# A hybrid decoder step: first block reordered, output projection's router and decode tile and the delta stage's decode products on column tiles

## The reference

```python
hn = rms_norm(x, norm1_g) * (1 + sc1) + sh1          # sh, sc, gt: silu(c) @ w_ada + b_ada
qkv, z, beta, alpha, u = split(hn @ w_in)
q, k, v = split(silu(causal_conv(qkv)))              # 4 heads of 128; q, k normalized
o, s_gdn = gdn_chunked(q, k, v, -exp(a_log) * softplus(alpha + dt_bias), sigmoid(beta), s0)
o_a = rms_norm(o) * silu(z)
y, x_s5 = s5_scan(u, x0, ...)                        # 32 groups of 64 complex states
y = gelu(y); o_b = rms_norm(y * sigmoid(y @ glu_w + glu_b))
x = x + gt1 * (concat(o_a, o_b) @ w_out)
hn = rms_norm(x, norm2_g) * (1 + sc2) + sh2
s = sigmoid(hn @ w_router)                           # 16 experts in 4 groups: best group, top 2 in it
x = x + gt2 * sum_e combine_e * (silu(hn @ w_gate_e) * (hn @ w_up_e)) @ w_down_e
y = rms_norm(x, final_g)
```

## Time and profile before

| | |
|---|---|
| time, median of 3 runs | 1298.97 us (1297.41 to 1302.08) |
| the profiled execution | 1299.72 us, its span 1298.0 us |
| granted PE clock, mean | 0.926 |
| busy: PE, PEld, DVE, ACT, POOL | 1121.2 (86%), 680.7 (52%), 552.8 (43%), 306.5 (24%), 230.6 (18%) us |

### The profile page before, as it was taken

One profiled execution on the slowest core, in us unless ns is written; L12 is line 12 of the kernel. 1 busy time (PEld: TensorE's weight loads), 2 busy tenths in 40 slices (PEclk: granted clock), 3 DMA queues, 4 the chain that ended last, 5 costly groups with the idle time before them and its releaser, 6 DMA issues. The chain is left out here.

```text
span 1298.0 us, 15179 instructions
## 1 busy us (share of the span) xinstructions
PE 1121.2 (86%) x5094; PEld 680.7 (52%) x5095; DVE 552.8 (43%) x1238; ACT 306.5 (24%) x684; POOL 230.6 (18%) x366
## 2 busy tenths in 40 slices
PE   4899997996996899688879799996499999889876
PEld 3466664444865677577764445543244444434332
DVE  3143357275365354697732432546411111111128
ACT  5121231051113333322214222232011111101123
POOL 0100000085403334211120000102311111101050
PEclk9899999997998996888889899997699999999988
DMA  9587061011015000375517100006377565797463
GB/s 349 167 245 259 1 258 65 1 66 65 14 26 132 2 1 1 126 282 172 171 33 284 66 17 32 33 33 156 101 259 259 166 216 172 243 319 262 146 258 149
DMA packets 127007, 181.95 MB, mean 140 GB/s; under 512 B 36685, under 2 KB 80450, under 8 KB 126942
## 3 DMA queue, kind: packets, MB, share of 16 engines
q1 hardware_dynamic: 115948, 146.96, 34.1%
q0 software_dynamic: 7376, 21.59, 5.0%
q10 hardware_dynamic: 3626, 12.64, 2.4%
HBM read 131.62 MB, written 48.47 MB: 139 GB/s over the span
## 5 line engine op out<-in xcount | busy, mean ns | idle before, releaser
L2128 PE MATMUL bank<-w_out,H 128*128 x384 | 173.4, 605 | 11.3 <-DMA w_out<-in_w_up 6.4
L368 PE MATMUL bank<-hT,w_ring 128*128 128x344 f32 x576 | 170.9, 459 | 3.8 <-ACT hT L552 3.8
L368 PEld LDWEIGHTS bank<-hT,w_ring 128*128 128x128 f32 x576 | 110.5, 193 | 62.6 <-issue 6.4
L2128 PEld LDWEIGHTS bank<-w_out,H 128*128 128x128 f32 x384 | 72.9, 193 | 109.2 <-issue 109.2
L2408 PE MATMUL bank<-w_out,hT 128*128 128x512 f32 (+1 forms) x288 | 127.5, 595 | 0.5 <-DVE hT L1920 0.5
L453 PE MATMUL bank<-w_ring,hT 128*128 128x512 f32 x256 | 115.1, 606 | 8.8 <-issue 8.8
L2192 DVE TENSOR_TENSOR H<-H,bank 128x256 f32<-128x256 f32 x24 | 10.1, 420 | 248.2 <-ACT H L2163 248.2
L2112 PE MATMUL bank<-y1T,H 128*128 x192 | 91.4, 620 | 10.6 <-DVE H L2201 7.9
L453 PEld LDWEIGHTS bank<-w_ring,hT 128*128 128x128 f32 x256 | 64.4, 256 | 55.1 <-issue 41.7
L2408 PEld LDWEIGHTS bank<-w_out,hT 128*128 128x128 f32 (+1 forms) x288 | 50.1, 179 | 64.5 <-issue 63.7
L2112 PEld LDWEIGHTS bank<-y1T,H 128*128 128x128 f32 x192 | 35.5, 195 | 52.3 <-issue 52.3
(11 more groups left out here) (523 smaller groups left out, 1797.3 us busy)
## 6 DMA issues: line engine op xcount, KB each, us to landing
ys_d<-ZO SPq DMA_DIRECT2D x18, 1024.0 KB, 13.1
y1T<-in_w_down SPq DMA_DIRECT2D x16, 1024.0 KB, 5.6
w_out<-in_w_gate SPq DMA_DIRECT2D x16, 1024.0 KB, 8.1
w_out<-in_w_up SPq DMA_DIRECT2D x16, 1024.0 KB, 11.5
ys_d<-H ACTq DMA_DIRECT2D x24, 512.0 KB, 5.4
w_ring<-in_w_in SPq DMA_DIRECT2D x4, 2048.0 KB, 8.2
y1T<-in_w_ada SPq DMA_DIRECT2D x4, 2048.0 KB, 8.1
hT<-in_w_ada SPq DMA_DIRECT2D x4, 2048.0 KB, 13.0
```

The source lines that it names most:

```text
L368: mm = t.matmul(ps[3 * (m % 2) + s][:, 0:SEG], w_ring[:, q % 2, k, (m % 4) * P:(m % 4 + 1) * P], hT[:, k, s * SEG:(s + 1) * SEG], start=(k ...
L2128: mm = t.matmul(ps[2 + p][:, :], xT[p][:, k, :], wgu[:, bass.ds(buf, 1), k, :].rearrange("p o n -> p (o n)"), start=(k == 0), stop=(k == K ...
```

## The change

*First block.* The second half of `powers` now follows the copies of the gate rows, and the first two phase tables are made ahead of the wait for the gates. *Delta stage.* `decode_product` takes all four heads at once; each head writes its own 32 partitions of bank 3 (a column tile of PE), and the loop runs over tokens outside, heads inside. Two calls take the place of four. ACT's `product_rows` first copies the four pieces to their places and then scales them. *Row products* become transposes. *Output projection.* The tiles go in the order 0, 1, 2, decode, 3 to 7. The router's eight products write four column tiles: the weights, loaded twice so that 32 columns are filled, are held and the tokens streamed; ACT copies the partial sums out (`lg_part`), and one product with `pick16` adds them and turns them back (`logits`), in the middle of the next half tile. The decode tile is made the same way, from the last 32 columns of `hT`, with `dec_part` and `pick_dec`; POOL makes the two pick matrices. Five groups of tiles are routed instead of four. The diff, cut to its core and moved eight columns to the left:

```diff
             elif m == 10:
                 powers(2, 6)
-            elif m == 11:
-                powers(6, LAGS + 1)
         pe.wait(v, "gate_rows")
         for x in range(3):
             dve.did(v.tensor_copy(gate_rows[:, x * SEG:(x + 1) * SEG], ps[x][:, 0:SEG]), "gate_rows")
+        powers(6, LAGS + 1)
         power_copies()
         eighth_angle()
+        tables(0)
+        tables(1)

         v.wait_ge(hp_land, 32)
         act.wait(v, "gates")
         dve.did(v.tensor_tensor(sp_t[:, 0], gates[:, :, 4:8], bc(hp[:, 0, :], [P, 9, HEADS], 1), ALU.add), "absx")

-        tables(0)
-        tables(1)
         tables(2)
         tables(3)
         act.wait(v, "ln")
...

-        def decode_product(col, hs, name):
-            for h in hs:
-                for b in range(DEC):
-                    mm = t.matmul(ps[3][0:DEC, h * P:(h + 1) * P], col[:, h, b, :], Sd[:, b, h, :], start=(b == 0), stop=(b == DEC - 1))
+        def decode_product(col, name):
+            for b in range(DEC):
+                for h in range(HEADS):
+                    mm = t.matmul(ps[3][32 * h:32 * h + DEC, 0:P], col[:, h, b, :], Sd[:, b, h, :], start=(b == 0), stop=(b == DEC - 1))
             pe.did(mm, name)
...
         t.wait_ge(s_in_land, 16 * DEC)
-        decode_product(kcol, (0, 1), "kS0")
+        decode_product(kcol, "kS")
         merge(0, 1)
-        decode_product(kcol, (2, 3), "kS")
         merge(0, 2)
         merge(0, 3)
...
             if c == 0:
                 act.wait(t, "kS")
-                decode_product(qcol, (0, 1), "qS0")
+                decode_product(qcol, "qS")
             elif c > 1:
...
                 pe.did(mm, f"o{c}_{l}")
-            if c == 0:
-                decode_product(qcol, (2, 3), "qS")
             merge(c + 1, 2)
             if 2 <= c < 6:
...
+        def product_rows(out, scales, name):
+            for h in range(HEADS):
+                act.did(a.activation(out[:, h * P:(h + 1) * P], ps[3][32 * h:32 * h + DEC, 0:P], ACT.Copy))
+            act.drain(a)
+            for h in range(HEADS):
+                act.did(a.activation(out[:, h * P:(h + 1) * P], out[:, h * P:(h + 1) * P], ACT.Identity, scale=scales[:, h:h + 1]), name)
...
                 pe.wait(a, "kS")
-                scaled(ud, 3, adb, "kS")
+                product_rows(ud, adb, "kS")
             if c + 1 < NT:
...
     sp.dma_start(X2[:, 0:NT, :], A["x_prompt"][0].rearrange("(i p) d -> p i d", p=P)).then_inc(land6, 16)
     sp.dma_start(X2[0:DEC, NT, :], A["x_sample"].rearrange("b o d -> (b o) d")).then_inc(land6, 16)
-    sp.dma_start(w_r[:, :, :], A["w_router"].rearrange("(k p) e -> p k e", p=P)).then_inc(rland, 16)
+    for n in range(2):
+        sp.dma_start(w_r[:, :, n, :], A["w_router"].rearrange("(k p) e -> p k e", p=P)).then_inc(rland, 16)
     sp.dma_start(b_r[:, :], A["b_router"].unsqueeze(0).to_broadcast([P, EXPERTS])).then_inc(rland, 16)
...
             src = A2[:, k, :] if b // 2 == 1 else modT[:, (GT1, None, SH2)[b // 2] + k, :]
-            mm = t.matmul(ps[6 + b % 2][:, (k % 4) * P:(k % 4 + 1) * P], src[:, 0:1].to_broadcast([P, P]), ident[:, :], start=True, stop=True)
+            mm = t.transpose(ps[6 + b % 2][:, (k % 4) * P:(k % 4 + 1) * P], src[:, 0:1].to_broadcast([P, P]), ident[:, :])
...
+w_r, lg_part = r6(P, KD, 2, EXPERTS), r6(P, P)
+pick16, pick_dec = r6(P, EXPERTS), r6(P, DEC)
...
-ROUTED = ((0, 1, 2), (3, 4, 5), (6,), (7, 8))
+ORDER = (0, 1, 2, NT, 3, 4, 5, 6, 7)
+ROUTED, PLACE = ((0, 1, 2), (NT,), (3, 4, 5), (6,), (7,)), (0, 3, 4, 7, 8)
+dec_part = H2[:, 7, :]
...
-        for i in range(9):
+        for i in ORDER:
             n = P if i < NT else DEC
-            if i == NT:
-                pe.wait(sp, "mix8_1")
+            if i == ORDER[8]:
+                pe.wait(sp, f"mix{i}_1")
                 for e in range(2):
                     load_gate_up(sp, e, e)
             dve.wait(sp, f"H2_{i}")
...
         for k in range(KD):
-            mm = t.matmul(ps[6][0:n, 0:EXPERTS], h2T[:, k, 0:n], w_r[:, k, :], start=(k == 0), stop=(k == KD - 1))
-        pe.did(mm, f"lg{i}")
+            j = 32 * (k % 4)
+            mm = t.matmul(ps[6][j:j + 32, 0:n], w_r[:, k, :, :].rearrange("p n e -> p (n e)"), h2T[:, k, 0:n], start=(k < 4), stop=(k >= 4))
+        pe.did(mm, f"lgp{i}")
+
+    def logits(t, i):
+        n = P if i < NT else DEC
+        act.wait(t, f"lgp{i}")
+        pe.did(t.matmul(ps[6][0:n, 256:256 + EXPERTS], lg_part[:, 0:n], pick16[:, :], start=True, stop=True), f"lg{i}")

...
+        t.wait_ge(rland, 48)
+        pool.wait(t, "picks")
+        for a, i in enumerate(ORDER):
             for half_ in range(2):
-                b = 2 * (i % 2) + half_
-                if i >= 2:
-                    dve.wait(t, f"mix{i - 2}_{half_}")
+                b, cols = 2 * (a % 2) + half_, slice(half_ * 512, (half_ + 1) * 512)
+                if a >= 2:
+                    dve.wait(t, f"mix{ORDER[a - 2]}_{half_}")
                 for k in range(KD):
-                    mm = t.matmul(ps[b][0:n, :], hT[:, k, i * P:i * P + n], w_out[:, k, half_ * 512:(half_ + 1) * 512], start=(k == 0), stop=(k == KD - 1))
-                pe.did(mm, f"mix{i}_{half_}")
-                if 2 * i + half_ in (0, 1, 2):
-                    decode_rows(2 * i + half_)
-                if half_ == 0 and i >= 2:
-                    route(t, i - 2)
-                    if i in (5, 8):
-                        ranks(t, (i - 5) // 3)
-            if i >= 1:
-                route_T(t, i - 1)
-        route(t, 7)
+                    if i < NT:
+                        mm = t.matmul(ps[b][:, :], hT[:, k, i * P:(i + 1) * P], w_out[:, k, cols], start=(k == 0), stop=(k == KD - 1))
+                    else:
+                        j = 32 * (k % 4)
+                        mm = t.matmul(ps[b][j:j + 32, :], hT[:, k, T - 32:T], w_out[:, k, cols], start=(k < 4), stop=(k >= 4))
+                    if half_ == 1 and a >= 2 and k == 3:
+                        logits(t, ORDER[a - 2])
+                pe.did(mm, f"mix{i}_{half_}" if i < NT else f"part{half_}")
+                if 2 * a + half_ in (0, 1, 2):
+                    decode_rows(2 * a + half_)
+                if half_ == 0 and a >= 2:
+                    route(t, ORDER[a - 2])
+                    if a in (5, 6):
+                        ranks(t, a - 5)
+            if a >= 1:
+                route_T(t, ORDER[a - 1])
+            if i == NT:
+                for half_ in range(2):
+                    act.wait(t, f"part{half_}")
+                    pe.did(t.matmul(ps[2 * (a % 2) + half_][0:DEC, :], pick_dec[:, :], dec_part[:, half_ * 512:(half_ + 1) * 512], start=True, stop=True), f"mix{i}_{half_}")
+        route(t, ORDER[7])
+        logits(t, ORDER[7])
         ranks(t, 2)
-        route_T(t, 8)
-        route(t, 8)
+        route_T(t, ORDER[8])
+        route(t, ORDER[8])
+        logits(t, ORDER[8])
         ranks(t, 3)
-        dve.wait(t, "pos3")
+        ranks(t, 4)
+        dve.wait(t, "pos4")
         pe.did(t.matmul(ps[5][:, 0:EXPERTS], ones_m[:, :], before[:, 9, :], start=True, stop=True), "total")
         moe_tensor(t)
         fin_tensor(t)
...
             n = P if i < NT else DEC
+            pe.wait(a, f"lgp{i}")
+            act.did(a.activation(lg_part[:, 0:n], ps[6][:, 0:n], ACT.Copy), f"lgp{i}")
             pe.wait(a, f"lg{i}")
-            act.did(a.activation(lg[0:n, i, :], ps[6][0:n, 0:EXPERTS], ACT.Sigmoid), f"lg{i}")
+            act.did(a.activation(lg[0:n, i, :], ps[6][0:n, 256:256 + EXPERTS], ACT.Sigmoid), f"lg{i}")

...
-                route_copy(i - 2)
-                scores(i - 2)
+            if at >= 2:
+                route_copy(ORDER[at - 2])
+                scores(ORDER[at - 2])
+            if i == NT:
+                for half_ in range(2):
+                    pe.wait(a, f"part{half_}")
+                    act.did(a.activation(dec_part[:, half_ * 512:(half_ + 1) * 512], ps[2 * (at % 2) + half_][:, :], ACT.Copy), f"part{half_}")
             dve.wait(a, f"x1_{i}")

...
-            for i in range(lo, hi):
-                tt(before[:, i + 1, :], before[:, i, :], cnt[:, i, :], ALU.add, f"cnt{r}")
+            for x in range(n):
+                tt(before[:, PLACE[r] + x + 1, :], before[:, PLACE[r] + x, :], cnt[:, lo + x, :], ALU.add, f"cnt{r}")
...
             for half_ in range(2):
-                b, c0 = 2 * (i % 2) + half_, half_ * 512
-                if half_ == 1 and i in (4, 7, 8):
-                    choose((4, 7, 8).index(i))
-                if half_ == 1 and i in (5, 8):
-                    place((i - 5) // 3)
+                b, c0 = 2 * (at % 2) + half_, half_ * 512
+                if half_ == 1 and at in (4, 5, 8):
+                    choose((4, 5, 8).index(at))
+                if half_ == 1 and at in (5, 6):
+                    place(at - 5)
                 pe.wait(v, f"mix{i}_{half_}")
```

(2 more changed lines are left out.)

39 lines of the change are left out of this document (20 added, 19 removed).

## The result

The changed kernel takes 1259.96 us (median of 4 runs, 1259.47 to 1263.78), the kernel before 1298.19 (4 runs beside it, 1295.0 to 1302.08): ratio 0.9711, 95% interval 0.9677 to 0.9744. The forecast was 1261, range 1250 to 1276. The profiled execution of the changed kernel has a span of 1257.9 us, 40.1 less than that of before; PE is busy for 1086.3 us (86%), 34.9 us less.

The account below looks back on a forecast made before the run. PE was read as the bound, with waits on DVE and ACT in the first block and DVE's chain at the tail. Terms -19.15 - 9.5 - 1.3 - 8.9 = -38.85 us against 1299.72 gave 1260.9, said as 1261, range 1250 to 1276.

Parts of the forecast that it names:

- gate rows ahead of the powers: First block: 18 small products leave the path to PE's next projections, -4.35 us; a gap of about 4.4 us stays.
- gap at the norm products: First block: with the phase tables made earlier, PE's wait falls from 11.84 to 1.2 us, -10.6.
- no slow clock behind it: First block, behind the norm products: without the gap PE's clock stays full, -4.2 us, bounds 0 and 4.4.
- decode products: Delta stage: two column-tile products replace four pieces, second chunk starts near 454.4 against 463.98, -9.5 us, bounds -11 and +1.
- row products ahead of the loop: Ahead of the output projection's loop: 24 row products become transposes, paced by ACT's evictions, -1.3 us, between 0 and 2.7.
- tail: Behind the last projection half: DVE's choices in one chain up to the totals' copy, 28.2 us, +8.0.
- scatters, until the first tile of the experts: Behind the routing: two scatters instead of four follow the last places, 1.25 us each, -2.5.
- The router: Output projection: eight products on four column tiles plus one sum, 1.70 us becomes 0.78, seven times, -6.4.
- The decode tile: Output projection: placed fourth on column tiles; a wait of some 3 us for ACT replaces the time saved, -5.2.
- The clock in the projection loop: Rival, chance 0.02: half clock after each router, half tiles 13.7 instead of 6.9 us; with twelve, 82 us lost, 1343.
- no wait took the place of the long one: Rival, chance 0.06: the wait at the norm products stays through the decays, costing 10.6 + 4.2 us, so 1276.
- the narrow products do overlap: Rival, chance 0.09, claimed the opposite: narrow column-tile matmuls in delta stage and router do not overlap, so 1281.

Follow-up runs that it names:

- the gate rows' kernel: Only the gate rows put ahead of the powers in the kernel before, tables still behind the gates: 1291.09 us, ratio 0.9944.
- the parts measured alone: One part each put into the kernel before: first block 1279.01 us, decode products 1287.16, output projection without row products as transposes 1290.64; row products not run alone.

## Why the prediction was right

The mechanisms were right in the main, and five of the eight steps came out within 1.3 us. That the sum was right to 1 us was also luck: the forecast steps gave 32.6 us instead of 38.85, and 7.5 us that no step forecast made up for it. Between the two profiles, in us:

| step | forecast | profiles |
|---|---|---|
| gate rows ahead of the powers | -4.35 | -4.47 |
| gap at the norm products | -10.6 | -10.59 |
| no slow clock behind it | -4.2 | -2.46 |
| decode products | -9.5 | -6.98 (B -4.21, C -2.77) |
| row products ahead of the loop | -1.3 | -0.5 |
| projection loop | -14.4 | -13.54 |
| tail | +8.0 | +6.69 |
| scatters, until the first tile of the experts | -2.5 | -0.74 |
| everything else | 0 | -7.5 |
| sum | -38.85 | -40.1 |

- *The gate rows.* Right, and the gate rows' kernel shows that the step pays by itself. Of the 1.9 us kept as a bound for the slow start, 0.4 came.
- *The tables.* Right: what is late next was ACT's own eviction, 1.25 us for the 1.2 said. "No gap, no slow clock" was the step that failed: 1.25 us of gap were left, the clock granted from the norm products on is 0.84 over 11 us where the forecast had 1.0, and 1.00 in the kernel with the norm products a tile later. The term measured 2.46 of 4.2.
- *The decode products.* The mechanism was right, and the ratio: 1.94 us at full clock against 7.32, 3.8 to one. The step that failed is "the second product 446.1 to 448.0": it took the clock for full. In six profiles of this code it took 2.20 to 3.60 us, by execution, and C was 10.8 to 12.3; the profile in the table above is the slowest of the six. The first chunk's start was said to be 4.4 us earlier against the rows before it, and was 4.2.
- *The row products.* Ahead of the loop this step took the clock for full. In all nine profiles with the transposes the granted clock there is 0.64 to 0.81, and the stretch takes 8.6 to 9.5 us; with matmuls it was 1.00 and 9.16 in four profiles, and in the fifth half clock began 0.4 us into it. Whether the transposes do it or the longer waits of a PE with less to do, no run tells apart.
- *The router.* 0.78 said, 0.72 measured. The change of mode cost some 0.1 us each, as said: a router starts 0.07 us before the half ahead of it ends (747.15 against 740.19 + 7.03), and the half behind it 0.06 us before the router ends; pieces of one mode overlap by 0.15. The Trainium skill, TensorEngine Tiling (Array Packing), Key Properties, says that a change of the tiling mode drains TensorE; in the trace the pieces still overlap across the change, and all that it shows of a cost is the smaller overlap.
- *The decode tile.* The wait of some 3 us for ACT was there, 2.99.
- *The clock in the projection loop.* The rival with 0.02 did not come: pieces of 8 records take 3.68 to 3.70 us behind routers, transposes and sums alike. The one fall in this loop is that of the decode tile, in six of ten profiles, 1.6 us. The Trainium skill, TensorE: Matmul & The Clock Gate, Part 4, says that transposes don't count as busy for the clock in the way matmuls do; here 24 more of them inside the dense loop did no harm, while the 24 ahead of it, between waits, go with a granted clock of 0.64 to 0.81.
- *The tail.* 28.2 us said, 27.84 measured. The term is 1.3 too large because today's tail was laid at 20.1 and is 21.15.
- *The scatters.* This step failed: it priced the issue (two times 1.25 us), and what the list waits for is the landing. The last scatter's issue did end 2.3 us sooner behind the copy, but the wait for its landing went from 1.34 to 2.60. The two scatters that went from the end were the decode tile's, with 8 tokens each; the last is now one of 128 tokens. In the seven profiles with this grouping of tiles that wait is 2.1 to 2.6 us, in the four with the old one 1.33 to 1.34, and the first product of the experts comes 11.4 to 12.3 us behind the copy instead of 13.1 to 13.2.
- *Everything else.* -1.4 ahead of the gate columns, -0.4 in the start of the projections, -2.8 in D beside the row products, -3.3 in the experts, +0.4 behind. By the table above D spreads by more than this without an edit in it. Whether a part of it is the change's, in the experts above all, the runs don't settle: the medians are 38.2 apart, the steps above add up to 32.6, and the parts measured alone to 38.6.

None of the other rivals came: no wait took the place of the long one, and the narrow products do overlap. Of the signs of being right, two missed: the clock at the norm products, which was said to be full, and the second decode product, 3.60 us for at most 3.5.

## What to carry to other kernels

Price a moved piece of work by what it hangs on, not by the clock time at which it stood: the tables came earlier by themselves as soon as PE did. Column tiles give nearly their whole factor even for 8 columns of weights, but a matmul piece that becomes short no longer covers the wait behind it, and here the work that came next then stood at half clock in seven profiles of seven. Shortening a chain only pays up to the next one of nearly the same length (lists landing behind the choice, masks in memory behind the norm products); look for it before the edit, and take several profiles of one kernel before a stage's few us are put down to an edit.

## What was not expected of the hardware

A gap of 1.25 us on PE, with small products on either side, was followed by half clock (16 products in 3.60 us instead of 1.95); with the gap filled by a projection tile they took 2.03. After waits of 2.67 and 2.89 us the same 16 matmuls took 7.13 and 10.17 us in two executions, and in the changed kernel 7.13 after 3.06: the length of a wait does not tell whether the clock falls. The landing of scatters did not take the same everywhere: the list's wait was 1.34 us behind a row of four that ended with two scatters of 8 tokens, 2.60 behind two of 128 tokens, and 4.27 where these two followed closely on four of 128 tokens. What they carry and what stands close ahead of them both differ here; which of the two counts was not tested.
